# The mixer's group norm: its steps spread over several heads in the first half, the last pair's sum ahead of them in the second

## The reference, cut to what matters

```python
y = y.reshape(b, L, SSD_WIDTH).astype(x.dtype) * jax.nn.silu(z)
y = rms_norm(y.reshape(b, L, SSD_GROUPS, SSD_WIDTH // SSD_GROUPS),
             ssd_norm.reshape(SSD_GROUPS, SSD_WIDTH // SSD_GROUPS)).reshape(b, L, SSD_WIDTH)
out = jnp.concatenate([fourier_mix(u_f, fourier_w), y], axis=-1) @ w_out
```

## Time and profile before

| what | us |
|---|---|
| three runs | 3715.21, 3721.26, 3727.25 |
| median | 3721.26 |
| the profiled execution, its own time | 3724.43 |
| its span, first to last instruction | 3723.1 |
| TensorE busy in the span | 3510.5 (94%) |
| VectorE, ScalarE, GpSimd busy | 1672.8, 1438.8, 1428.4 |

### The profile page before, as it was taken

One profiled execution on the slowest core, in us unless ns is written; L12 is line 12 of the kernel. 1 busy time (PEld: TensorE's weight loads), 2 busy tenths in 40 slices (PEclk: granted clock), 3 DMA queues, 4 the chain that ended last, 5 costly groups with the idle time before them and its releaser, 6 DMA issues.

```text
span 3723.1 us, 45249 instructions
## 1 busy us (share of the span) xinstructions
PE 3510.5 (94%) x17424; PEld 2796.0 (75%) x17424; DVE 1672.8 (45%) x2997; ACT 1438.8 (39%) x2448; POOL 1428.4 (38%) x651
## 2 busy tenths in 40 slices
PE   6899999998799998999999999999998999999998
PEld 4788889785578886866676778887876766778886
DVE  7976463546420115845442243133754453234143
ACT  3223354554432223344443344343343443334342
POOL 3554433321244444334323444444333333344443
PEclk9999999999899998999999999999999999999999
DMA  7574355221122332212212222323222222223332
GB/s 300 193 248 145 126 160 166 69 86 51 46 74 91 102 91 81 90 62 82 78 64 91 86 79 89 103 90 110 82 72 71 71 74 89 76 85 95 98 95 81
DMA packets 118423, 376.45 MB, mean 101 GB/s; under 512 B 15424, under 2 KB 16320, under 8 KB 117952
## 3 DMA queue, kind: packets, MB, share of 16 engines
q1 hardware_dynamic: 107280, 356.33, 29.6%
q10 hardware_dynamic: 10928, 17.22, 1.6%
HBM read 359.86 MB, written 2.10 MB: 97 GB/s over the span
## 4 chain that ended last, share of the span: by engine, by line
PE 76%; DVE 11%; ACT 5%; issue 3%; POOL 2%; DMA 2%; ACTq 1%; SPq 0%; DVEq 0%; POOLq 0%
PE ps L1333 23%; PE ps L1334 22%; PE ps L1335 22%; DVE b L2194 2%; ACT b L1660 2%; PE ps L1576 1%; POOL b L2558 1%; PE ps L1597 1%; ACTq L1766 1%; PE ps L1558 1%; DVE b L2230 1%; PE ps L1631 1%; PE ps L1620 1%; PE ps L1554 1%; DVE b L2460 1%
## 5 line engine op out<-in xcount | busy, mean ns | idle before, releaser
L2558 POOL TENSOR_TENSOR b<-b,b 128x1024 fp32r<-128x1024 f32 (+2 forms) x579 | 1324.3, 2287 | 2183.2 <-ACT b L1660 2166.5
L1333 PE MATMUL ps<-b,b 128*128 128x512 f32 (+3 forms) x4848 | 1842.4, 380 | 75.1 <-POOL b L2558 29.2
L1334 PE MATMUL ps<-b,b 128*128 128x512 f32 (+3 forms) x4848 | 1803.4, 372 | 0.0
L1335 PE MATMUL ps<-b,b 128*128 128x512 f32 (+3 forms) x4848 | 1801.9, 372 | 0.0
L1333 PEld LDWEIGHTS ps<-b,b 128*128 128x128 f32 x4848 | 935.0, 193 | 309.7 <-issue 118.7
L1335 PEld LDWEIGHTS ps<-b,b 128*128 128x128 f32 x4848 | 934.1, 193 | 160.1
L1334 PEld LDWEIGHTS ps<-b,b 128*128 128x128 f32 x4848 | 935.4, 193 | 154.8 <-issue 5.1
L1660 ACT ACTIVATE b<-b 128x1024 fp32r<-128x1024 f32 (+2 forms) x622 | 607.4, 978 | 388.5 <-PE ps L1335 247.4
L2109 DVE SCALAR_TENSOR_TENSOR b<-ps,b,b 128x511 f32<-128x511 f32 x88 | 66.0, 750 | 365.0 <-ACT b L1711 365.0
L2194 DVE CUSTOM_DVE_ANT_0 b<-b,b,b 128x1024 bf16<-128x1024 f32 x112 | 218.7, 1953 | 16.1 <-DMA b<-in_ada 4.1
L1721 ACT ACTIVATE b<-b 128x512 fp32r<-128x512 f32 (+1 forms) x110 | 64.8, 590 | 397.4 <-DVE b L2118 294.7
(11 more groups left out here) (231 smaller groups left out, 2337.4 us busy)
## 6 DMA issues: line engine op xcount, KB each, us to landing
b<-in_w SPq DMA_DIRECT2D x458, 512.0 KB, 3.5
b<-in_ada SPq DMA_DIRECT2D x88, 512.0 KB, 5.2
b<-in_w SPq DMA_DIRECT2D x80, 384.0 KB, 3.1
b<-in_w SPq DMA_DIRECT2D x80, 320.0 KB, 2.9
b<-b ACTq DMA_DIRECT2D x176, 64.0 KB, 2.0
b<-in_const SPq DMA_DIRECT2D x24, 256.0 KB, 3.8
b<-in_x SPq DMA_DIRECT2D x1, 2048.0 KB, 16.4
out<-b SPq DMA_DIRECT2D x8, 256.0 KB, 2.5
```

What stands on the lines that cost most here:

```text
L1333: pe.matmul(out, a[0], b[0], start=first, stop=False)
L1334: pe.matmul(out, a[0], b[1], start=False, stop=False)
L1335: return pe.matmul(out, a[1], b[0], start=False, stop=last)
L2558: then(pool.tensor_tensor(wlo[j % NS][:, 0:nk * w], raw[j % NR][:, 0:nk * w], whi[j % NS][:, 0:nk * w].bitcast(F32), ALU.subtract), "lop", j)
```

## The change

`groupnorm` is replaced by a helper `gnorm(hf, *steps)` that makes any list of the five kinds of steps, and the steps are placed one by one:

- First half: all three `gn1` behind pair 2's `yv`; both `gn2` and `gn3` behind head 9's steps; all `gn4` and `gn5` behind pair 3's `yv`. Pair 2's head steps thus move ahead, directly behind pair 1's `yv`.
- Second half: `gn2` and `gn3` of group 0 and then pair 5's `yv` come ahead of tile 2's K-steps 0 to 4; then `gn1` of tile 2, `gn2` and `gn3` of group 1, and `gn4` and `gn5` of tile 0; then K-step 5 of the three tiles; then `gn4` and `gn5` of tiles 1 and 2.
- `gn2` writes in bank 6 and no longer takes one of the banks 0 to 5.

No instruction is added or removed. The engines' programs themselves are unchanged.

```diff
-    def groupnorm(hf, o):
-
-        own = (0, 1) if o == 0 else (2,)
-        done = (0,) if o == 0 else (1, 2)
-        return ([do("gn1", hf=hf, o=x) for x in own] + [do("gn2", hf=hf, o=o), do("gn3", hf=hf, o=o)]
-                + [do("gn4", hf=hf, o=x) for x in done] + [do("gn5", hf=hf, o=x) for x in done])
+    def gnorm(hf, *steps):
+
+        return [do(kind, hf=hf, o=o) for kind, o in steps]
...
         if h % 2 == 0 and k > 0:
-            B += [do("yv", k=k - 1)] + (groupnorm(0, k - 2) if k in (2, 3) else [])
-            if k == 5:
-                B += groupnorm(1, 0)[:2]
+            B.append(do("yv", k=k - 1))
+            if k == 3:
+                B += gnorm(0, ("gn1", 0), ("gn1", 1), ("gn1", 2))
+            elif k == 4:
+                B += gnorm(0, ("gn4", 0), ("gn4", 1), ("gn4", 2), ("gn5", 0), ("gn5", 1), ("gn5", 2))
+            elif k == 5:
+                B += gnorm(1, ("gn1", 0), ("gn1", 1))
+        if h == 9:
+            B += gnorm(0, ("gn2", 0), ("gn3", 0), ("gn2", 1), ("gn3", 1))
...
     F = fore()
     part(F, tiles[2], range(5))
+    S += gnorm(1, ("gn2", 0), ("gn3", 0)) + [do("yv", k=5)] + weave(F)
+    S += gnorm(1, ("gn1", 2), ("gn2", 1), ("gn3", 1), ("gn4", 0), ("gn5", 0))
+    F = fore()
     for t in tiles:
         part(F, t, range(5, 6))
-    S += weave(F, groupnorm(1, 0)[2:] + [do("yv", k=5)] + groupnorm(1, 1), 1.1)
+    S += weave(F) + gnorm(1, ("gn4", 1), ("gn4", 2), ("gn5", 1), ("gn5", 2))
...
         elif k == "gn2":
-            s["bank"] = gn_bank = take()
+            s["bank"] = 6
             mark("gp", s["hf"], s["o"])
         elif k == "gn3":
-            s["bank"] = gn_bank
-            held[gn_bank] = False
+            s["bank"] = 6
```

## The result

| | before | after |
|---|---|---|
| median of 9 runs each, us | 3720.78 | 3706.94 |
| lowest and highest, us | 3710.05, 3727.25 | 3699.24, 3715.49 |
| ratio to before | | 0.9965 (95%: 0.9952 to 0.9978) |
| profiled execution: span, us | 3723.1 | 3703.0 |
| stretch from the last `z` product to `wo`'s fourth tile, us | 94.85 | 78.76 |

The forecast was 3708 with a gain of 13.2 us, and the range 3700 to 3716 holds the result. The interval of the ratio reaches from 8 to 18 us of gain, so that the runs alone don't place it beyond 0.3%. The profiled spans differ by 20.1 us; 16.1 of these lie in the stretch; the other 4 are 4.8 us the other way ahead of it and 8.8 us behind it, where the two kernels do the same.

A forecast was written before the change was run, and what follows sets the result against it. TensorE, busy 3510.5 of 3723.1 us, was taken as the bound, so gains come only from its idle time and clock. Gains of 9.3 and 3.9 us sum to 13.2, giving 3721.26 - 13.2 = 3708 us, range 3700 to 3716.

The forecast's parts named there:

- Step 1: Up to pair 2 and `fo1`: new 2.0 us TensorE stop on `z`'s last tile; 0.7 and 2.2 us squares waits go.
- Step 2: Fourier end: `fo3` waits 0.9 us, 5.2 us wait for head 10's `es` goes, `wo`'s first K-step at 930.75 against 940.47.
- Step 3: First half's norm consumed at once: stops of 2.2 and 1.9 us before K-steps 1 and 2; gain so far 9.3 us.
- the collision: VectorE's first norm subtraction waits for GpSimd to end: 2 us taken, ends nothing to 3 us.
- Step 4: From pair 5's `u1` to K-step 6: 13.5 us instead of 17.4, gain 3.9 us, with a 2.75 us wait before K-step 5.
- If these run at 1.2 GHz: Second half: tiles 1 and 2 hide behind the three K-steps 5 at the lower clock; K-step 6 starts at 966.1.
- the far end: Extreme value of an uncertain term; for the second half's end, 2.3 us better if the clock stays up.
- Bank 6: `gn2`'s bank costs nothing: pair 2's sum leaves it at 910.0, `gn2` comes at 918.8; any lag would count in full.
- The table load: ScalarE's second first-half `gn3`: load priced 1.28 us; the skill page's extra 1.38 us drain would make the gain 11.8 us.
- Held back: New stops at `z`'s last tile, `fo2`'s copies and GpSimd's subtractions cost more: gain 7.5 us, 3714; chance 18%.
- It does nothing: The path through the six pairs sets the end, pair 5's `u1` stays at 963: gain 0 to 4 us, 3719; chance 6%.
- The clock rival: Clock falls at the 895.7 stop and stays down through `fo1`, to 928: 12 us slower, 3733; chance 6%.

The follow-up runs named there:

- e12: Changed kernel with an empty step behind pair 1's sum and both first-half norm sums and factors ahead of head 8's `md`: 3710.69 us, ratio 0.9970 to before.
- e6: Changed kernel with the first half's `gn4` of tiles 1 and 2 moved behind tile 0's split, using two empty steps: 3709.42 us, ratio 0.9974 to before.
- e4: Changed kernel with tile 0's `gn4` and `gn5` ahead of group 1's factor (`gn3`) in the second half: 3705.52 us, ratio 0.9961 to before.
- e2: Kernel before with only the second half's new order and bank 6: 3716.44 us, ratio 0.9986 to before.
- e3: Kernel before with only the norm's sums put in bank 6: 3720.39 us, ratio 0.9998 to before.
- e5: Changed kernel with one empty step behind pair 1's sum in the background list: 3714.76 us, ratio 0.9989 to before.
- e1: Changed kernel with the second half's steps in the order of before, so only the first half changed: 3713.89 us, ratio 0.9980 to before.
- e7: Changed kernel with the next weight chunk taken up ahead of the finished tile's copy and square: 3702.54 us, ratio 0.9958 to before.
- e8: Changed kernel with the edits of e4 and e7 together: 3702.97 us, ratio 0.9952 to before.
- e10: Changed kernel with the table load of the first half's second factor written twice; the second was not in the program: 3710.80 us, ratio 0.9976 to before.
- e13: Changed kernel with the edits of e8 and e12 together: 3697.23 us, ratio 0.9940 to before.

## Why the prediction was right, step by step

*Step 1.* The bank of `z`'s last tile gave a stop of 1.89 us (forecast 2.0), and VectorE read that tile right before. The squares' waits in the first half are gone. Right in place and size. e12 adds that removing the stop gains only about 1 us at the first K-step; where the rest goes was not followed.

*Step 2.* 0.74 us before `fo3` (forecast 0.9), no wait for head 10. The first K-step gained 8.75 us (46.85 to 38.10) against 9.7 less restarts.

*Step 3.* Stops of 1.78 and 1.18 us before K-steps 1 and 2 (forecast 2.2 and 1.9). VectorE's three subtractions beside GpSimd took 3.68 us. Two in a row took 1.47 us at 969.87, so three would take 2.1 at most, and the collision cost about 1.6 us (forecast 2):

```profile
939.07 3.68 DVE L2395 TENSOR_TENSOR b<-b,b 128x512 fp32r<-128x512 f32 x3
```

e6 shows what this means: VectorE's work there is the limit, not its order. The end of pair 5's `u1` moved from 69.63 to 59.58 us behind the last `z` product: 10.05 us of gain, forecast 9.3.

*Step 4.* The wait before K-step 5 was 2.69 us (forecast 2.75), and e4 shows its cause, the copy behind the factor: with the two exchanged it is gone. From the end of pair 5's `u1` to K-step 6 it took 12.65 us instead of 17.38: a gain of 4.7 us where the prediction had 3.9. Another 1.3 us, from K-step 6 to the fourth tile (6.53 instead of 7.84), the sum didn't have at all, nor the 1.6 us that go back behind the stop for GpSimd, which grew to 2.07 us. So step 4 gave 4.4 us in all. The term that was mis-sized is the clock. "If these run at 1.2 GHz" did not come true for the three K-steps 5 in the changed kernel's profile: they ran at full clock and left 0.48 us of wait, so that a clock that stayed up gave 0.8 us to K-step 6, where the far end had 2.3. It did come true in e2 and e12, and there K-step 6 has no wait.

*Bank 6* costs nothing by itself (e3). The sentence "If it were late, that lag would stand on the path in full" was written of pair 2's sum. In e5 the bank was late for another reader, the first group's logarithm, and TensorE stood for 3.3 us.

*The table load.* In the changed kernel the logarithm stands directly behind the second load, with nothing else to wait for:

```profile
929.20 1.28 ACT L1932 ACT_TABLE_LOAD   x1
930.50 0.69 ACT L1934 ACTIVATE b<-ps,b 128x512 f32<-128x512 f32 x1
```

1.30 us from load to logarithm. That alone says little of a switch, because the norm's first `gn3` had loaded the same table 8.7 us earlier, with no other load between. But earlier in the same profile ScalarE changes to and fro between an exponential (L1873) and a SiLU (L1749), with a load before each:

```profile
795.40 1.28 ACT L1873 ACT_TABLE_LOAD   x1
796.70 0.18 ACT L1873 ACTIVATE b<-ps 128x12 f32<-128x12 f32 x1
...
797.62 1.28 ACT L1749 ACT_TABLE_LOAD   x1
798.92 0.42 ACT L1749 ACTIVATE b<-b 128x256 f32<-128x256 f32 x1
```

1.30 us each again. The drain of 1.38 us that the Trainium skill's page "ScalarE: Activation LUTs", section "What ACT_TABLE_LOAD costs", adds to a switch isn't there, and the gain of 11.8 us that would have followed from it was not the one to take.

*The rivals.* "Held back" had the right places, but the far ends didn't come together. "It does nothing" is ruled out: the end of pair 5's `u1` moved by 10.05 us. The clock rival fell for the stretch it named: 1.00 from 902.6 to 939. But it was no idle thought: the same 1.9 us stop stands in e1, e4, e6, e7, e8 and e10 too, and in e1 and e7 the clock fell behind it.

```profile
897.61 1.34 PE L1441 MATMUL ps<-b,b 128*128 128x512 f32 x2 [1.89 <-DVE b L2152]
898.88 3.37 PE L1513 MATMUL ps<-b,b 128*64 128x128 f32 x32
902.09 1.91 PE L1525 MATMUL ps<-b,b 128*64 128x128 f32 x32
```

L1513 is `u1`'s first half, 3.37 us here against 1.97 in the changed kernel. The first K-step came at +39.84 and +39.68 in these two, and at +38.04 to +38.20 in the five others: 1.6 to 1.8 us for each such fall, against the 1.8 us that the prediction set as the far end. It came back within one `u1`. The forecast took 0 for this term, and the changed kernel's profile had 0; with five of seven kernels that way, part of it is luck.

Of the 14.5 us up to the 16th product the prediction had 13.2, and it had named the waits well; the clock's share, 4.7 us, it counted piece by piece. How much of that share belongs to the change and how much to chance stays open. Busy time up to that product differs by 2.5 us from kernel to kernel (70.6 to 73.1 us among after, e4, e6, e7, e8, e10, e12 and e13), and all eight lie 3.5 us or more under the 76.6 of before. That goes with their fewer and shorter stops, but no run here parts the two.

## What to carry to other kernels

When engines work fixed queues, replay those queues from the place where the orders part, with durations from the trace, and look at each bank and each copy for who is ahead of it: this found the new stops before the run, the 1.9 and 2.7 us ones with their sizes to about 0.1 us, the two before K-steps 1 and 2 (1.8 and 1.2 us) within 0.7. A step must be placed against the other engine's steps, not by its place in a list: an empty step cost 9 us, because it put the first factor behind two copies and the second between two others, and about half of that was the lower clock behind the waits. And measure such a change by its stretch in the profile, with TensorE's busy and idle time apart, and end the stretch where the clock is up again: the end chosen here left out 1.6 us of the changed kernel. The times need many runs for what one profile shows.

## What the runs showed of the hardware that was not expected

A stop of 1.9 us was followed by the lower clock in two of seven kernels and not in the others, with the same instructions around it. The stop of 2.7 us before K-step 5 was followed by it in e2, e5 and e12, and not in the changed kernel, e6, e7 and e10. In the kernel before, a stop of 2.16 us was followed by it. A stop of 3.06 us there, before the product at 878.79, was not. The stop before the fourth tile was 2.06 to 2.17 us in six kernels (after, e2, e5, e6, e10, e12), and all six ran the next products at 1.2 GHz; it was 1.04 us or less in the other seven, and none did. So the length of the stop alone doesn't tell. One fall cost 1.5 to 1.8 us.

A second preload of the same table directly behind the first left no instruction in the profile (e10).
